# A two-block kernel on one core: the latent branch's projection as split products, its gating in pairs, and what moves between VectorE, ScalarE and GpSimd with it

## The chip, the cores and the metric

The kernel runs on one NeuronCore of a Trainium2 chip. The metric is the device time of one execution in microseconds (us); a measured time is the median of several runs. The engines are TensorE (PE in the rows; PEld is its weight load), VectorE (DVE), ScalarE (ACT), GpSimd (POOL) and SyncE (SP), which issues the transfers of weights. Each runs its own list of instructions in order and waits for the others on semaphores.

## What is computed

The reference runs two transformer blocks, one after the other, on 256 tokens of width 1024, all in float32. The part that the change touches is the mixer of the first block:

```python
proj = u @ w_in                                   # also g, the gates
o_a = dense_attention(q, k_a, v_a)                # latent branch, 8 heads of 64
o_b = dilated_mixture(qd, kd, vd)                 # dilated branch, 8 heads of 64
gates = sigmoid(g + b_gate)                       # 2 x 1024 per token
merged = gates[:, :, 0] * (o_a @ w_branch_a) + gates[:, :, 1] * (o_b @ w_branch_b)
mix = merged @ w_out
```

Before it stand a feed-forward block (SwiGLU) and the projections of the mixer; behind it a norm, a second feed-forward block, and then the second block with its own mixer of three branches.

## The kernel before

**Layout.** Activations lie transposed: 128 rows of a chunk of features by 256 tokens, eight chunks for the width. Weights come from one stream of tiles of 128 x 1024 floats (512 KB), which SP loads into a ring of six slots; a slot is loaded again when its tile has been used (`tiles_used`). The order of the stream is a list (`weight_order`). In the mixer it is: sixteen gate tiles `g1`, the four tiles `wb` of the dilated branch (the first of them ahead of the last gate tile), the four tiles `wa` of the latent branch, eight tiles `out1`, and then the feed-forward weights.

**Split products.** Nearly every product is made as three faster ones: each operand x is written as an upper part (x rounded to fp32r) and a lower part (x minus the upper), and `split_product` (L632 to L634) does upper by upper, upper by lower, lower by upper. Of a weight tile ScalarE makes the upper (`weight_upper`, L1546) into a place of its own, and GpSimd the lower (`weights_lower`, L2873), which it leaves in the ring. A table of places (`SPLIT_PLACE`) says where uppers go, and GpSimd walks the tiles in the order of the stream. The latent branch's four tiles `wa` are not split before the change: L994 multiplies whole float32 operands, four products for each of the eight chunks of 256 tokens.

**The head loop.** Sixteen heads (0 to 7 dilated, 8 to 15 latent) are worked in a software pipeline beside the sixteen gate tiles; step k of it handles gate tile k and head k. On PE a pair of steps is: gate tile 2n (24 products), the scores of heads 2n+2 and 2n+3 (L925), which wait until ScalarE has read the scores of the pair before (`exps`), the transposes of head 2n (L936), which wait for its probabilities (`probs`), the values of the pair before (L952), gate tile 2n+1, transposes of head 2n+1. On VectorE step k is: reciprocal of the sums of head k and scaling of its two halves of probabilities (`normalise`, L2392 and L2394), gate tile times the norm's inverse (L2429), the maxima of head k+2 (L2385, L2386), and in odd steps from 3 on the outputs of two heads out of PSUM (L2403 as a lower part for heads 0 to 7, L2406 as a copy for 8 to 15). On ScalarE: for heads 0 to 7 their upper parts, tanh of the gate (L1723), a weight upper or two (L1546), the copy of the transposes of head k (`turned`, L1704), and the exponentials of head k+2 (`exps`, L1696). The dilated branch's four projections are woven into the end of it (`dilated_branch`), each over a whole bank of 512 columns.

**The latent branch.** When the last dilated tile is done, PE works off eight products of 256 columns, m1_0 to m1_7, in two alternating banks. VectorE reads each with its gate (L2449), adds it to the dilated branch's chunk (L2452), and one chunk behind that makes the lower part for the next product (L2295), whose upper part ScalarE has made (L1553). PE then starts `out1`, the product with `w_out`: eight tiles of 24 products (192), where each chunk k of the first tile waits for the k-th pair of parts of `merged` (`input_parts`).

**GpSimd's order there.** After the lowers of all `g1` and `wb` tiles it sums the squares of the context's norm (`context_sums`, L2927 and L2928, three operations of 512 columns and one of 256), then makes the lowers of the eight `out1` tiles. The first use of the sum is behind the third `out1` tile on PE.

## Time and profile before

| | |
|---|---|
| median of 3 runs | 1250.64 us (1243.90 to 1254.69) |
| profiled execution | 1251.45 us |
| its span in the trace | 1249.8 us, 24409 instructions |
| PE, DVE, ACT, POOL busy | 95%, 68%, 51%, 44% of the span |
| mean granted clock of TensorE | 0.982 |

Times in the rows are us from the start of the span. A row of a timeline is: start, duration, engine, line and operation, out<-in, how many were merged into it, and in brackets the idle time ahead of it and what ended it. The durations of PE's rows overlap, since its products are pipelined; the distance of two starts is what one costs. A row of the windows is: the stretch, its length, for each engine busy time and number of instructions, the granted clock of TensorE (1.00 is 2.4 GHz, 0.50 is 1.2 GHz), the share of the DMA engines and GB/s.

### The profile page before, as it was taken

What the parts mean: (1) busy time and instruction counts of PE and PEld (TensorE: products, weight loads), DVE (VectorE), ACT (ScalarE), POOL (GpSimd) and SP (SyncE); (2) the same over time, 40 slices, a digit from 0 to 9 for tenths busy, and PEclk for the clock granted to TensorE, in tenths of its full rate; (3) what the DMA queues carried; (4) which work ended last, traced back from release to release, by engine and by line L of the source; (5) the groups of instructions that cost most, each with busy time, mean ns of one, the idle gap of its engine ahead of it and who ended that gap; (6) DMA issues with size and microseconds to landing.
All of it is one profiled execution on the core that took longest, in us unless ns stands there. A gap on an engine that the chain in (4) does not pass through costs nothing.

```text
span 1249.8 us, 24409 instructions
## 1 busy us (share of the span) xinstructions
PE 1193.5 (95%) x9116; PEld 1115.9 (89%) x9116; DVE 849.3 (68%) x1142; ACT 635.5 (51%) x1020; POOL 553.2 (44%) x287
## 2 busy tenths in 40 slices
PE   6999998999999999999999999998999999999998
PEld 6999998976888999999999888987777899999998
DVE  6798984864986567777554852688745686656555
ACT  5534446525773454545445546466425634655553
POOL 0355656732455433443435644468530384222331
PEclk9999998999999989999989999998999999999999
DMA  8677764433334547788514334232323264565653
GB/s 314 229 279 279 264 233 135 152 101 119 104 117 135 169 169 255 283 286 285 188 49 152 119 101 129 75 102 84 102 68 101 85 179 142 172 195 189 187 189 111
DMA packets 58096, 207.04 MB, mean 166 GB/s; under 512 B 6576, under 2 KB 8240, under 8 KB 57776
## 3 DMA queue, kind: packets, MB, share of 16 engines
q1 hardware_dynamic: 49824, 177.23, 43.4%
q0 software_dynamic: 6912, 25.17, 5.7%
q10 hardware_dynamic: 1296, 3.74, 0.8%
q8 instruction: 45, 0.74, 0.2%
q14 instruction: 19, 0.16, 0.0%
HBM read 205.07 MB, written 1.05 MB: 165 GB/s over the span
## 4 chain that ended last, share of the span: by engine, by line
PE 61%; DVE 19%; issue 6%; ACT 6%; POOL 4%; DMA 3%; DVEq 0%; SPq 0%; POOLq 0%; ACTq 0%
PE psum L632 17%; PE psum L633 16%; PE psum L634 16%; DVE parts L2143 4%; DMA low<-stream 3%; POOL own_parts L2873 2%; POOL high L2956 2%; DVE high L2174 1%; PE psum L771 1%; PE psum L925 1%; PE psum L643 1%; PE psum L645 1%; ACT parts L1477 1%; PE psum L657 1%; PE psum L644 1%
## 5 line engine op out<-in xcount | busy, mean ns | idle before, releaser
L632 PE MATMUL psum<-parts 128*128 128x256 f32 x1584 | 443.9, 280 | 19.7 <-DVE parts L2143 9.8
L633 PE MATMUL psum<-parts 128*128 128x256 f32 x1584 | 446.6, 282 | 0.0
L634 PE MATMUL psum<-parts 128*128 128x256 f32 x1584 | 442.5, 279 | 0.0
L632 PEld LDWEIGHTS psum<-parts 128*128 128x128 f32 x1584 | 300.3, 190 | 22.9 <-issue 16.7
L2881 POOL TENSOR_TENSOR parts<-low,parts 128x1024 fp32r<-128x1024 f32 x60 | 169.0, 2817 | 340.2 <-ACT parts L1477 340.2
L633 PEld LDWEIGHTS psum<-parts 128*128 128x128 f32 x1584 | 300.3, 190 | 0.0
L634 PEld LDWEIGHTS psum<-parts 128*128 128x128 f32 x1584 | 300.1, 189 | 0.0
L1477 ACT ACTIVATE parts<-low 128x1024 fp32r<-128x1024 f32 x198 | 205.5, 1054 | 129.3 <-DMA low<-stream 127.8
L2873 POOL TENSOR_TENSOR own_parts<-low,parts 128x1024 fp32r<-128x1024 f32 x75 | 184.5, 2472 | 166.9 <-ACT parts L1546 166.6
L2143 DVE TENSOR_TENSOR parts<-low,parts 128x1024 fp32r<-128x1024 f32 x138 | 178.9, 1331 | 23.3 <-ACT parts L1477 22.8
L633 PE MATMUL psum<-u_parts,parts 128*128 128x256 f32 (+1 forms) x560 | 164.5, 294 | 0.0
L634 PE MATMUL psum<-scratch_parts,own_parts 128*128 128x256 f32 (+1 forms) x496 | 149.6, 302 | 0.0
L2873 POOL TENSOR_TENSOR own_parts<-low,single_upper 128x1024 fp32r<-128x1024 f32 x36 | 88.9, 2474 | 82.1 <-ACT single_upper L1546 79.5
L633 PEld LDWEIGHTS psum<-u_parts,parts 128*128 128x128 f32 x560 | 107.7, 192 | 2.1
L634 PE MATMUL psum<-late_parts,own_parts 128*128 128x256 f32 x360 | 101.0, 281 | 0.0
L634 PEld LDWEIGHTS psum<-scratch_parts,own_parts 128*128 128x128 f32 x496 | 95.8, 193 | 3.7
L632 PE MATMUL psum<-late_parts,parts 128*128 128x256 f32 x320 | 92.6, 290 | 4.3 <-DVE u_parts L2283 3.1
L632 PE MATMUL psum<-scratch_parts,single_upper 128*128 128x256 f32 (+1 forms) x256 | 79.5, 311 | 6.9 <-POOL own_parts L2873 5.7
L1546 ACT ACTIVATE parts<-low 128x1024 fp32r<-128x1024 f32 x75 | 78.4, 1050 | 14.3 <-DMA low<-stream 14.3
L633 PE MATMUL psum<-u_parts,single_upper 128*128 128x256 f32 (+1 forms) x280 | 83.3, 298 | 0.0
L2174 DVE SCALAR_TENSOR_TENSOR high<-high,low 128x1024 f32<-128x1024 f32 x64 | 79.1, 1275 | 0.0
L2149 DVE TENSOR_TENSOR parts<-low,parts 128x256 fp32r<-128x256 f32 x66 | 54.9, 831 | 31.9 <-ACT parts L1483 31.9
(369 smaller groups left out, 2122.4 us busy)
## 6 DMA issues: line engine op xcount, KB each, us to landing
low<-stream SPq DMA_DIRECT2D x334, 512.0 KB, 3.5
high<-conditioning POOLq DMA_DIRECT2D x48, 512.0 KB, 5.1
high<-wuq ACTq DMA_DIRECT2D x1, 1152.0 KB, 11.2
low<-x SPq DMA_DIRECT2D x4, 256.0 KB, 5.8
high<-ctx ACTq DMA_DIRECT2D x1, 1024.0 KB, 5.6
out<-low SPq DMA_DIRECT2D x8, 128.0 KB, 1.8
low<-cst ACTq DMA_DIRECT2D x1, 850.5 KB, 4.9
low<-vec ACTq DMA_DIRECT2D x1, 157.5 KB, 5.7
```

Source lines behind the costliest of these rows:

```text
L632: pe.matmul(out, w_hi[:, cols_], x_hi, start=start, stop=False, **kw)
L633: pe.matmul(out, w_hi[:, cols_], x_lo, start=False, stop=False, **kw)
L634: return pe.matmul(out, w_lo[:, cols_], x_hi, start=False, stop=stop, **kw)
L643: pe.matmul(out, hi(k, n), w_hi[:, cols_], start=k == 0, stop=False)
L1477: act.activation(ring_hi[:, j % RING, :], ring[:, t % RING, :], ACT.Copy)\
L1546: act.activation(weight_place(t), ring[:, t % RING, :], ACT.Copy)\
L2143: dve.tensor_tensor(ring_lo[k][:, j % RING, :], ring[:, t % RING, :], ring_hi[:, j % RING, :], ALU.subtract).then_inc(S("lower_ready"), 1)
L2149: dve.tensor_tensor(hidden_lo[k][:, par, :], hidden[:, par, :], hidden_hi[k][:, par, :], ALU.subtract).then_inc(S("hidden_split"), 1)
L2174: dve.scalar_tensor_tensor(out=acc_, in0=cond_places[g], scalar=small[:, bass.ds(i * 2 + who, 1)], in1=acc_, op0=ALU.mult, op1=ALU.add).th ...
L2873: pool.tensor_tensor(tile_lo[:, t % RING, :], ring[:, t % RING, :], weight_place(t), ALU.subtract).then_inc(S("weights_split"), 1)
L2881: pool.tensor_tensor(ring_lo[k][:, j % RING, :], ring[:, t % RING, :], ring_hi[:, j % RING, :], ALU.subtract).then_inc(S("lower_ready_2"), 1)
L2956: pool.affine_select(out=a, in_=a, compare_op=ALU.is_ge, fill=NEG, base=0, pattern=[[-sgn * P, 2], [sgn, T]], channel_multiplier=-sgn)\
```

## The change

- The tiles `wa` are split: they get places 29 to 32 for their uppers (where the latent queries and keys stood), ScalarE makes four more uppers and GpSimd four more lowers, and one function `head_branch` now projects either branch with split products, two chunks into one bank. The eight banks m1_0 to m1_7 become four, wa_0 to wa_3.
- The outputs of heads 8 to 15 are split too: ScalarE writes their upper parts (`head_upper_1`), VectorE subtracts instead of copying.
- Gating, adding, uppers and lowers of the merged chunks go in pairs of 512 columns. The add's wait for its own result ahead of the lower is gone.
- For heads 12 to 15 ScalarE scales the probabilities (`normalised`, in steps 11 to 14 between tanh and the weight upper); VectorE only takes the reciprocal, behind the maxima of head k+2.
- GpSimd makes the context's sums in two pieces: two operations behind the lower of gate tile 12, the others behind the lower of the first `wb` tile. Ahead of the lower of the second `out1` tile it waits until three of the four pairs are merged.
- The gate rows before tanh lie in a buffer of their own (`gated_rows`), and two semaphores for memsets become one.

The diff, cut to its core:

```diff
 for tiles, places in (...
-                      (tiles_between(("g1", GATES_1[0]), ("wb", 3)), (5, 4) * 5 + (5, 26, 27, 4, 5, 28, 26, 27, 4, 5)),
+                      (tiles_between(("g1", GATES_1[0]), ("wa", 3)),
+                       (5, 4) * 5 + (5, 26, 27, 4, 5, 28, 26, 27, 4, 5, 29, 30, 31, 32)),
...
-            def dilated_branch(pair):
+            def head_branch(m, pair):
...
-                    pe.wait_ge(S("outs_copied"), 8)
-                w = split_weights(AT[("wb", pair)])
+                    pe.wait_ge(S("outs_copied"), 8 if m == "wb" else 16)
+                w = split_weights(AT[(m, pair)])
...
-            for n in range(8):
-                name = f"m1_{n}"
-                bank_free(pe, name)
-                w = tile_wait(AT[("wa", n // 2)])
...
-                    mm = pe.matmul(bank(name)[:, 0:T], w[:, (n % 2 * 4 + k) * P:(n % 2 * 4 + k + 1) * P], oa[:, k, :],
-                                   start=k == 0, stop=k == 3)
+            for pair in range(4):
+                head_branch("wa", pair)
...
+            def normalised(k):
+                x = 2 * (k % 2)
+                act.wait_ge(S("inverse_sums"), k - 11)
+                for j in range(2):
+                    act.activation(prob[:, k % 2, j, :], prob[:, k % 2, j, :], ACT.Identity, scale=rden[:, x + j:x + j + 1])\
+                       .then_inc(S("probs"), 1)
...
-                if k in (3, 5, 7, 9):
+                if k % 2 and k > 1:
...
+                if 10 < k < 15:
+                    normalised(k + 1)
...
-            merged_upper(merged1, "merged1", {0: [AT[("out1", 0)]], 1: [AT[("out1", 1)]], 3: [AT[("out1", 2)]],
-                                                7: [AT[("out1", 3)]]})
+            weight_upper(AT[("wa", 1)])
+            weight_upper(AT[("wa", 2)])
+            head_upper_1(14)
+            head_upper_1(15)
+            weight_upper(AT[("wa", 3)])
+            for pair in range(4):
+                if pair < 3:
+                    weight_upper(AT[("out1", pair)])
+                act.wait_ge(S("merged"), 2 * pair + 2)
+                act.activation(p1_hi[:, 2 * pair:2 * pair + 2, :], merged1[:, 2 * pair:2 * pair + 2, :], ACT.Copy)\
+                   .then_inc(S("input_uppers"), 2)
+            weight_upper(AT[("out1", 3)])
...
             for k in range(16):
-                normalise(k)
+                if k < 12:
+                    normalise(k)
...
                 if k < 14:
                     maxima(k + 2)
+                if 10 < k < 15:
+                    inverse_sums(k + 1)
...
+            for pair in range(4):
+                name, own = f"wa_{pair}", slice(2 * pair, 2 * pair + 2)
                 product_ready(dve, name)
...
+                dve.tensor_tensor(merged1[:, own, :], merged1[:, own, :], latent_gated, ALU.add).then_inc(S("merged"), 2)
+                if pair:
+                    merged_lower_1(pair - 1)
+            dve.wait_ge(S("merged"), 8)
+            merged_lower_1(3)
...
-            weights_lower(AT[("cq", 0)] + 5, AT[("wb", 3)])
-            context_sums()
-            weights_lower(AT[("out1", 0)], AT[("out1", 7)])
+            weights_lower(AT[("cq", 0)] + 5, AT[("g1", GATES_1[12])])
+            context_sums(1, 3)
+            weights_lower(AT[("g1", GATES_1[13])], AT[("wb", 0)])
+            context_sums(3, 5)
+            weights_lower(AT[("g1", GATES_1[15])], AT[("out1", 0)])
+            pool.wait_ge(S("merged"), 6)
+            weights_lower(AT[("out1", 1)], AT[("out1", 7)])
```

How ScalarE's list reads in steps 11 and 12 of the head loop. Before (L1723 is tanh, L1546 a weight upper, L1704 the copy of the transposes, L1696 the exponentials, L1431 a square of the context):

```order
L1723 ACTIVATE high<-high,low 128x256
L1546 ACTIVATE parts<-low 128x1024
L1704 ACTIVATE high<-psum 128x512
L1696 ACTIVATE high,low<-psum,low 128x256 x2
L1431 ACTIVATE low<-high 128x512
L1723 ACTIVATE high<-high,low 128x256
L1546 ACTIVATE single_upper_65<-low 128x1024
```

And now (L1726 is tanh, L1707 the upper parts of two latent heads, L1713 the scaling of a head's probabilities, L1542 a weight upper):

```order
L1707 ACTIVATE heads_latent_upper<-psum 64x256 x2
L1726 ACTIVATE high<-high,low 128x256
L1713 ACTIVATE high<-high,low 128x256 x2
L1542 ACTIVATE parts<-low 128x1024
L1700 ACTIVATE high<-psum 128x512
L1692 ACTIVATE high,low<-psum,low 128x256 x2
L1427 ACTIVATE low<-high 128x512
L1726 ACTIVATE high<-high,low 128x256
L1713 ACTIVATE high<-high,low 128x256 x2
L1542 ACTIVATE single_upper_65<-low 128x1024
```

The scaling of a head stands between tanh and the weight upper, so ahead of the exponentials on which PE's next scores wait.

The end of VectorE's part in the merge, from the last gating of the dilated branch on. Before, the last three of eight chunks (L2449 gates, L2452 adds, L2295 makes the lower part):

```order
L2449 SCALAR_TENSOR_TENSOR high<-high,psum 128x256
L2452 TENSOR_TENSOR high<-high 128x256
L2295 TENSOR_TENSOR u_parts<-high,late_parts 128x256
L2449 SCALAR_TENSOR_TENSOR high<-high,psum 128x256
L2452 TENSOR_TENSOR high<-high 128x256
L2295 TENSOR_TENSOR u_parts<-high,late_parts 128x256 x2
```

Now, the last two of four pairs (L2483 gates, L2487 adds, L2473 makes the lower part):

```order
L2483 SCALAR_TENSOR_TENSOR high<-high,psum 128x512
L2487 TENSOR_TENSOR high<-high 128x512
L2473 TENSOR_TENSOR u_parts<-high,late_parts 128x512
L2483 SCALAR_TENSOR_TENSOR high<-high,psum 128x512
L2487 TENSOR_TENSOR high<-high 128x512
L2473 TENSOR_TENSOR u_parts<-high,late_parts 128x512 x2
```

The same three kinds of operation, half as many and twice as wide; the last two lowers still stand behind the last add.

GpSimd's list from the lowers of gate tiles 11 and 12 on. Before (L2873 is a weight lower, L2927 and L2928 are the context's sums; the last row is the eight `out1` tiles):

```order
L2873 TENSOR_TENSOR own_parts<-low,single_upper_63 128x1024
L2873 TENSOR_TENSOR own_parts<-low,single_upper_64 128x1024
L2873 TENSOR_TENSOR own_parts<-low,parts 128x1024 x2
L2873 TENSOR_TENSOR own_parts<-low,single_upper_65 128x1024
L2873 TENSOR_TENSOR own_parts<-low,single_upper_63 128x1024
L2873 TENSOR_TENSOR own_parts<-low,single_upper_64 128x1024
L2873 TENSOR_TENSOR own_parts<-low,parts 128x1024 x2
L2927 TENSOR_TENSOR low<-low 128x512 x3
L2928 TENSOR_TENSOR low<-low 128x256
L2873 TENSOR_TENSOR own_parts<-low,parts 128x1024 x8
```

And now, from behind the lower of gate tile 12 on (L2908 is a weight lower, L2962 and L2964 the sums, single_upper_66 to 69 the tiles `wa`):

```order
L2962 TENSOR_TENSOR low<-low 128x512 x2
L2908 TENSOR_TENSOR own_parts<-low,parts 128x1024 x2
L2908 TENSOR_TENSOR own_parts<-low,single_upper_65 128x1024
L2962 TENSOR_TENSOR low<-low 128x512
L2964 TENSOR_TENSOR low<-low 128x256
L2908 TENSOR_TENSOR own_parts<-low,single_upper_63 128x1024
L2908 TENSOR_TENSOR own_parts<-low,single_upper_64 128x1024
L2908 TENSOR_TENSOR own_parts<-low,parts 128x1024 x2
L2908 TENSOR_TENSOR own_parts<-low,single_upper_66 128x1024
L2908 TENSOR_TENSOR own_parts<-low,single_upper_67 128x1024
L2908 TENSOR_TENSOR own_parts<-low,single_upper_68 128x1024
L2908 TENSOR_TENSOR own_parts<-low,single_upper_69 128x1024
```

The sums stand ahead of seven weight lowers of the head loop instead of behind them, and the four new lowers stand ahead of `out1`.

## Rows read from the trace of the kernel before

**Rows 1.** The page: busy time of the engines; the chain by engine

```profile
PE 1193.5 (95%) x9116; PEld 1115.9 (89%) x9116; DVE 849.3 (68%) x1142; ACT 635.5 (51%) x1020; POOL 553.2 (44%) x287
PE 61%; DVE 19%; issue 6%; ACT 6%; POOL 4%; DMA 3%; DVEq 0%; SPq 0%; POOLq 0%; ACTq 0%
```

**Rows 2.** Timeline of PE: latent projection, first and last tiles of out1

```profile
393.35 5.99 PE L994 MATMUL psum<-high,low 128*128 128x256 f32 x27
...
400.84 1.99 PE L994 MATMUL psum<-high,low 128*128 128x256 f32 x8 [0.42 <-DVE high L2449]
403.79 5.45 PE L994 MATMUL psum<-high,low 128*128 128x256 f32 x24 [0.96 <-DVE high L2449]
408.89 0.47 PE L632 MATMUL psum<-late_parts,parts 128*128 128x256 f32 x1
...
411.88 0.38 PE L632 MATMUL psum<-late_parts,parts 128*128 128x256 f32 x1
...
428.05 0.28 PE L634 MATMUL psum<-late_parts,own_parts 128*128 128x256 f32 x1
...
432.56 0.28 PE L634 MATMUL psum<-late_parts,own_parts 128*128 128x256 f32 x1
```

**Rows 3.** The chain in order of time: part of the latent projection

```profile
393.51 3.47 PE psum L994 x16
```

**Rows 4.** Timeline of VectorE and GpSimd in the merge

```profile
389.55 0.69 DVE L2413 SCALAR_TENSOR_TENSOR high<-high,psum 128x512 f32<-128x512 f32 x1 [2.54 <-PE psum L634]
393.55 0.69 DVE L2413 SCALAR_TENSOR_TENSOR high<-high,psum 128x512 f32<-128x512 f32 x1 [2.10 <-PE psum L634]
397.53 0.42 DVE L2452 TENSOR_TENSOR high<-high 128x256 f32<-128x256 f32 x1
397.99 2.47 DVE L2295 TENSOR_TENSOR u_parts<-high,late_parts 128x256 fp32r<-128x256 f32 x1
400.82 2.13 DVE L2452 TENSOR_TENSOR high<-high 128x256 f32<-128x256 f32 x1
...
388.04 4.01 POOL L2927 TENSOR_TENSOR low<-low 128x512 f32<-128x512 f32 x3
...
397.63 5.04 POOL L2873 TENSOR_TENSOR own_parts<-low,parts 128x1024 fp32r<-128x1024 f32 x2 [4.77 <-ACT parts L1546]
405.67 2.45 POOL L2873 TENSOR_TENSOR own_parts<-low,parts 128x1024 fp32r<-128x1024 f32 x1 [3.00 <-ACT parts L1546]
```

**Rows 5.** Timeline of the head loop, steps 13 and 14: VectorE, GpSimd, PE

```profile
374.10 4.70 DVE L2394 TENSOR_SCALAR high<-high,low 128x256 f32<-128x256 f32 x2
373.86 4.79 POOL L2873 TENSOR_TENSOR own_parts<-low,single_upper 128x1024 fp32r<-128x1024 f32 x2 [2.58 <-ACT single_upper L1546]
378.86 0.66 PE L936 MATMUL psum<-low,high 128*128 128x128 f32 x4 [1.03 <-DVE high L2394]
```

**Rows 6.** Timeline of the head loop, step 11: ScalarE, VectorE, GpSimd, PE

```profile
362.49 0.51 ACT L1723 ACTIVATE high<-high,low 128x256 f32<-128x256 f32 x1 [1.37 <-DVE high L2429]
362.90 1.04 ACT L1546 ACTIVATE parts<-low 128x1024 fp32r<-128x1024 f32 x1
363.08 0.58 DVE L2386 TENSOR_SCALAR low<-low 128x2 f32<-128x2 f32 x1
361.20 2.44 POOL L2873 TENSOR_TENSOR own_parts<-low,parts 128x1024 fp32r<-128x1024 f32 x1
365.39 1.99 PE L925 MATMUL psum<-high 96*128 96x256 f32 x8 [0.18 <-ACT high L1696]
```

**Rows 7.** Windows: TensorE's granted clock around gaps in its work

```profile
777.00:780.60 3.60, 1.77 (x16) 1.57 (x14) 2.27 (x2) 3.59 (x6) 1.24 (x2) 1.00 0.20 35
780.60:784.00 3.40, 3.40 (x16) 3.17 (x17) 0.00 (x0) 0.63 (x1) 2.35 (x1) 0.50 0.29 117
376.00:380.00 4.00, 2.97 (x26) 2.45 (x27) 3.93 (x6) 0.83 (x4) 2.65 (x2) 1.00 0.59 170
210.50:217.40 6.90, 4.24 (x20) 4.27 (x21) 6.22 (x14) 4.65 (x10) 6.27 (x8) 0.51 0.01 2
```

More of the change, by code:

```diff
@@ L267 @@
                  24: HEADS_M, 25: ARENA_2["ys"][0],
-                 26: ARENA_1["qd"][0], 27: ARENA_1["kd"][0], 28: ARENA_1["vd"][0]}
+                 26: ARENA_1["qd"][0], 27: ARENA_1["kd"][0], 28: ARENA_1["vd"][0],
+                 **{29 + i: ARENA_1["q"][0] + i * TILE for i in range(4)}}
 assert SINGLE_PLACES[18] + TILE <= ARENA_2["t0"][0]
@@ L302 @@
           + ["wb_0", f"g1_{GATES_1[15]}", "wb_1", "wb_2", "wb_3"]
-          + [f"m1_{n}" for n in range(8)]
+          + [f"wa_{n}" for n in range(4)]
           + ["rows", "mk0"] + [f"mq{n}" for n in range(4)] + ["ish"]
@@ L324, in tile_of @@
 def tile_of(name):
-    for m in ("g1_", "g2_", "wb_"):
+    for m in ("g1_", "g2_", "wb_", "wa_"):
         if name.startswith(m):
@@ L330, in tile_of @@
         return AT[("uk", 0)]
-    if name.startswith("m1_"):
-        return AT[("wa", int(name[3:]) // 2)]
     if name == "rows":
@@ L2921, in link, with context_sums @@
                 pool.wait_ge(S("pool_steps"), steps[0])
-            def context_sums():
-                for i in range(1, 4):
+            def context_sums(first, last):
+                for i in range(first, min(last, 4)):
                     pool.wait_ge(S("squares"), SQ_BASE["ctx"] + i + 1)
                     link(pool.tensor_tensor(tmp[:, 0:2, :], tmp[:, 0:2, :], tmp[:, 2 * i:2 * i + 2, :], ALU.add))
-                pool.tensor_tensor(tmp[:, 0, :], tmp[:, 0, :], tmp[:, 1, :], ALU.add).then_inc(S("square_sums_2"), 1)
+                if last == 5:
+                    pool.tensor_tensor(tmp[:, 0, :], tmp[:, 0, :], tmp[:, 1, :], ALU.add).then_inc(S("square_sums_2"), 1)
             pool.wait_ge(S("cond_ready"), 1)
```

101 lines of the change are left out of this document (54 added, 47 removed).

## The prediction

> **What bounds the kernel now.** I read the page first: PE is busy 95% of the span, and the chain runs through it for 61% and through VectorE for 19% [rows 1]. So a microsecond counts only where it shortens PE's list or a wait in it. Next the timeline of PE around the latent projection [rows 2]: it starts at 393.35, the first `out1` product at 408.89, the second `out1` tile at 411.88. From there PE runs to the last product of the eighth tile at 432.56 without a wait of note. What costs time here is thus the projection (15.54 us), the first tile behind it (2.99 us), and the waits in the head loop ahead of it. Of these I look at two: 1.03 us at 378.86 [rows 5] and 0.18 at 365.39 [rows 6]. Then the timelines of VectorE and GpSimd [rows 4], because the same operation of VectorE takes 0.42 us once and 2.13 another time. Last the windows for TensorE's clock [rows 7].
>
> **How VectorE and GpSimd share.** L2452 and L2295, 256 columns with both inputs in SBUF, take 0.42 us when GpSimd is idle. At 397.99 L2295 took 2.47, at 400.82 L2452 took 2.13: each ended 0.3 us behind the GpSimd operation that was running. The operation at 389.55, 512 columns with one input in PSUM, took its 0.69 us in the middle of GpSimd's sums [rows 4]. With two GpSimd operations back to back (373.86, 4.79 us) two scalings on VectorE took 4.70 us together: one gets through at the end of each GpSimd operation [rows 5]. I take this as the rule of the sum: an SBUF-only operation of VectorE waits for the end of the GpSimd operation under way, and the next GpSimd operation goes ahead of the next VectorE one.
>
> **The change part by part.**
>
> *Projection.* 96 split products replace 32 float32 ones. One split product costs 4.51/39 = 0.116 us (40 starts from 428.05 to 432.56 [rows 2]), a tile of 24 costs 2.77, the four 11.1 us. The float32 ones stand in the trace as 64 instructions of 3.47/16 = 0.217 [rows 3], 13.9 us, and their phase took 15.54 with its waits. The weights are there in time: the uppers of `wa` need about 1 us of ScalarE each (1.04, L1546 [rows 6]) and the lowers 2.4 to 2.5 us of GpSimd (2.45, L2873 [rows 4]), less than the 2.77 a tile takes on PE, and GpSimd can start on them where the sums began, at 388.04 [rows 4], so the fourth is done by 398.1 and is asked for at 393.35 + 3 x 2.77 = 401.7. Banks are read within 1 us of a tile's end. So 11.1 - 15.54 = **-4.4 us**. Bounds: -2.8 if only the passes are saved (11.1 - 13.9), -4.4 if the waits go too.
>
> *Merge in pairs.* Here the gain is put at risk. I count from the end of the third `wa` tile. VectorE starts 0.2 us behind a tile's end (the last dilated tile frees PE at 393.35 [rows 2], its gating starts at 393.55 [rows 4]). Gating and adding 512 columns cost 0.69 each (the row at 389.55 has 512 columns). So: gating 0.2 to 0.9, adding to 1.6. That is three pairs merged, and it releases GpSimd, which has had the uppers of its next two tiles waiting. VectorE's next operation, the lower of pair 1, is already issued and goes first, to 2.2; GpSimd's lower of `out1` tile 1 runs from 2.1 to 4.5. The fourth tile ends at 2.77, its gating (PSUM, free) at 3.7. The add needs both inputs from SBUF and waits: 4.5, done 5.05. GpSimd goes on with tile 2, 4.9 to 7.3; the lower of pair 2 waits for it, done 7.85. ScalarE has by then copied the upper of pair 3 (5.1 to 5.7) and made the upper of tile 3 (to 6.7), so GpSimd goes on with it, 7.7 to 10.1, and the lower of pair 3 is done at 10.65. PE ends its first `out1` tile six products later, at 11.4. From its start at 2.77 that is 8.6 us, of which 3.8 and 2.1 are waits, against 2.99 before: **+5.6 us**. Bounds: were GpSimd idle, the chain would be 0.2 + 0.69 + 0.69 + 0.7 + 0.7 us long, then six products, 3.8 us in all, **+0.8 us**; the upper bound is the one above, since after the fourth lower nothing is left to collide. I take the upper one: it is what the rows give in order.
>
> *Head loop, step 11.* In step 11 PE's scores at 365.39 wait for ScalarE: tanh at 362.49, weight upper at 362.90, copy, exponentials [rows 6]. Two scalings of 256 columns now stand behind that tanh, 0.41 us each as tanh itself (362.49 to 362.90). They also wait for the reciprocal, which stands behind the maxima of head 13. The last operation of those, L2386 at 363.08, ended at 363.66 with GpSimd's operation, not after its own 0.17 us or so [rows 6]; GpSimd now stands in the two sums that were put there. They take 1.3 us each (4.01/3 [rows 4]): from 361.3 to 363.95. Reciprocal to 364.1, scalings to 364.95, and the weight upper starts 2.05 us later than at 362.90. PE's scores come **+2.05 us** later. Without the collision (L2386 done at 363.25) it would be +1.4. The upper parts of heads 8 and 9 go into ScalarE's idle 1.37 us ahead of tanh, at no cost; if that cover were gone, 0.8 us. Queued behind ScalarE's new wait are the weight upper, the copy and the exponentials, in this order.
>
> *Head loop, step 14.* The scalings of head 14 on VectorE, 4.70 us beside GpSimd [rows 5], were what PE's transposes at 378.86 waited for. The wait shows as 1.03 us behind a product drawn with 0.28, which frees PE after 0.12; so **-1.2 us**. ScalarE has these scalings done some 3 us before PE asks. What is late next is nothing I can find: the lower of gate tile 15, by the same count, comes 1 to 2 us ahead of its use.
>
> *Sums on GpSimd.* They leave the stretch in front of `out1`, where their 4.7 us covered nothing, since `wa` was not split; their result is used behind the third `out1` tile. The four new lowers take their place. Nothing from it but what stands above.
>
> *TensorE's clock.* A gap of 1.83 us on PE ending at 780.38 was followed by 3.4 us at 0.50, 1.2 GHz; the gap of 1.03 us ending at 378.86 was not, 1.00 all through [rows 7]. The waits of 3.8 and 2.1 us in the first `out1` tile lie above it. While PE has work at 1.2 GHz it does half of it, so one such stretch costs 3.4/2 = **+1.7 us**. Bounds: 0, and 3.4 for a stretch as long as at 210.50 (6.9 us) [rows 7]. The Trainium skill (TensorE: Matmul & The Clock Gate, "What's actually happening") says that the half clock is the state at rest and that activity lifts it, and its table has it return after idleness. A strict reading, that only unbroken idleness brings it, would make this term fall away for gaps of 2 us; the trace disagrees, a gap of 1.83 us was enough.
>
> **The sum.** -4.4 + 5.6 + 2.05 - 1.2 + 1.7 = +3.8 us on the profiled 1251.45, 1255.3. The median shown is 0.8 below the profiled execution, so 1254.5 us. Nothing behind 432.56 changes but the moment at which it starts. About 1% (12.5 us) is what a measurement of this kernel can tell from no change; this is 0.3%, no change by that bound.
>
> **The rivals.**
>
> *GpSimd and VectorE do not fall into step.* For it: the upper of `out1` tile 3 is ready only 0.6 us before GpSimd could take it, and a VectorE operation that is issued at once may go first. Against it: 4.70 beside 4.79 us [rows 5]. Then the first tile takes 3.8 us, no clock stretch comes: -4.4 + 0.8 + 2.05 - 1.2 = -2.8, 1247.9 us by the median. If the reciprocal is not held up either, 0.65 less, 1247.2. The Trainium skill (SBUF — State Buffer, "Practical consequences") says that issue order decides who holds the ports, not the kind of operation; by that, whoever is issued first at each release decides between this rival and the forecast.
>
> *The gap in the head loop lowers the clock too.* PE would wait at 365.4 for 0.2 + 2.05 us, more than the 1.83 of rows 7. Another 3.4 us at half clock, +1.7: 1256.2 us.
>
> *ScalarE becomes the bound of the last steps (the slower side).* The scaling of each of heads 12 to 15 waits on a reciprocal behind VectorE's maxima, which wait for PE's scores, and delays the uppers, copies and exponentials behind it. I have charged one head. If all four delay PE by 2.05 and each brings a clock stretch of 1.7, that is 4 x 3.75 = 15 instead of 2.05, so +16.8, 1267.5 us. It decides once ScalarE has no idle time left in a step; it has 1.37 us in step 11 [rows 6], and its wait at tanh is for VectorE, which gets lighter. That speaks against it.
>
> *The change does not do what it says*: PE waits for the lowers of `wa`, and the projection takes 15.5 as before. Then +4.4: 1258.9 us. The 3.6 us in hand, worked out above, speak against it.
>
> **How the numbers follow.** Forecast 0.50; not in step 0.28; the gap with a clock stretch 0.13; ScalarE the bound 0.05; the rest 0.04. The range must hold the forecast, the first rival and the second, and the spread of executions (1243.90 to 1254.69 before, whose median may lie 2 us off): 1246 to 1260 leaves out the slowest rival and some of the spread. Faster by over 1% needs more than all gains without a loss (-4.4 - 1.2): 0.03. Slower by over 1% is ScalarE as the bound and a little more: 0.06. The rest, 0.91, is within 1%.
>
> **What would show it.** In the profile after: the projection on PE from its first to the first `out1` product some 11.1 us long, without float32 pairs. The last two lowers of the merge on VectorE over 2 us each, beside three GpSimd lowers back to back, and waits of PE in the first `out1` tile of about 3.8 and 2.1 us. PE's wait for the scores of heads 14 and 15 about 2 us, none ahead of the transposes of head 14. A clock of 0.50 for 3.4 us or more behind the merge. The prediction is wrong if the last two lowers take 0.7 us each, or if the wait for the scores stays below 1 us, or if ScalarE is late in steps 12 to 14 too.

## The result, and the profile after

The changed kernel takes 1255.32 us (median of 22 runs, 1250.16 to 1264.48), beside 1250.64 us for the kernel before (22 runs, 1241.80 to 1256.39). The ratio is 1.0041, its 95% interval 1.0023 to 1.0059. So the change costs 0.2 to 0.6% and is no difference by the bound of 1%; forecast were 1254.5 us and no change.

The profiled execution of the changed kernel took 1252.21 us. Its page, the busy times, the chain by engine, and the group of split products that wait for the merged chunks:

```profile
span 1249.3 us, 24483 instructions
PE 1189.1 (95%) x9148; PEld 1114.7 (89%) x9148; DVE 834.7 (67%) x1122; ACT 647.0 (52%) x1036; POOL 544.1 (44%) x291
PE 69%; DVE 13%; ACT 6%; issue 5%; POOL 4%; DMA 2%; DVEq 0%; POOLq 0%; SPq 0%; ACTq 0%
L634 PE MATMUL psum<-late_parts,parts 128*128 128x256 f32 x320 | 93.3, 291 | 9.3 <-DVE u_parts L2473 5.1
```

The span is 0.5 us shorter than before, although the runs are slower, and PE is busy 4.4 us less [rows 1]. Whoever compares these two totals alone reads a gain. The stages say where the error lies: PE's first product of the mixer starts at 207.4 us here and at 213.2 before, 5.8 us earlier, though nothing ahead of it was changed. Across the profiled executions of all kernels of this study, with the same code up to there, the mixer starts between 207.4 and 214.0. One profile can't be compared with another by its span when what is looked for is 4 us. I therefore read stage against stage. The last row gives the place: 5.1 us of PE's idle time in that group was ended by L2473, the lower part of the merged chunks.

**The latent branch.** The timeline of PE; what is named L632 before is L634 here.

```profile
388.08 0.28 PE L634 MATMUL psum<-heads_latent_upper,single_upper 128*128 128x256 f32 x1
...
399.17 0.28 PE L634 MATMUL psum<-late_parts,parts 128*128 128x256 f32 x1
...
404.29 0.39 PE L634 MATMUL psum<-late_parts,parts 128*128 128x256 f32 x1 [3.57 <-DVE u_parts L2473]
...
407.05 0.58 PE L634 MATMUL psum<-late_parts,parts 128*128 128x256 f32 x1 [1.52 <-DVE u_parts L2473]
...
408.50 0.41 PE L634 MATMUL psum<-late_parts,parts 128*128 128x256 f32 x1
```

The projection takes 399.17 - 388.08 = 11.09 us instead of 15.54 [rows 2], 4.45 less, and PE does not wait in it. The first `out1` tile, 24 products, takes 408.50 - 399.17 = 9.33 us. From one start to the next it is 3.85 us ahead of 404.29 and 1.93 ahead of 407.05.

How long the tile took before has to be counted, and [rows 2] can mislead: its row at 411.88 is not the second tile but the last chunk of the first. Between 408.89 and 411.88 stand only 21 products. The second tile starts three products later, and 24 products behind that the third:

```profile
412.33 0.28 PE L632 MATMUL psum<-late_parts,parts 128*128 128x256 f32 x1
...
415.12 0.28 PE L632 MATMUL psum<-late_parts,parts 128*128 128x256 f32 x1
```

So the first tile took 412.33 - 408.89 = 3.44 us before, not the 2.99 of the prediction, and it now takes 5.89 us more.

What it waits for, in the timelines of VectorE and GpSimd over the same time:

```profile
397.99 0.69 DVE L2473 TENSOR_TENSOR u_parts<-high,late_parts 128x512 fp32r<-128x512 f32 x1
399.37 0.69 DVE L2483 SCALAR_TENSOR_TENSOR high<-high,psum 128x512 f32<-128x512 f32 x1 [0.70 <-PE psum L636]
400.15 1.33 DVE L2487 TENSOR_TENSOR high<-high 128x512 f32<-128x512 f32 x1
401.40 5.59 DVE L2473 TENSOR_TENSOR u_parts<-high,late_parts 128x512 fp32r<-128x512 f32 x2
...
398.20 2.73 POOL L2908 TENSOR_TENSOR own_parts<-low,parts 128x1024 fp32r<-128x1024 f32 x1 [4.88 <-DVE high L2487]
400.89 2.79 POOL L2908 TENSOR_TENSOR own_parts<-low,parts 128x1024 fp32r<-128x1024 f32 x1
403.65 2.80 POOL L2908 TENSOR_TENSOR own_parts<-low,parts 128x1024 fp32r<-128x1024 f32 x1
```

The three GpSimd operations end at 400.93, 403.68 and 406.45. VectorE's three operations with both inputs in SBUF end at 401.48, 404.2 and 406.99, each half a microsecond behind one of them: one gets through per operation of GpSimd. The gating at 399.37, with one input in PSUM, takes its 0.69 in the middle of such an operation. The lower at 397.99, issued 0.2 us ahead of GpSimd's first, takes 0.69 too. That agrees with what the Trainium skill says of issue order (SBUF — State Buffer, "Who interferes with whom"): the operation that issues first is not held up.

**The head loop.** The timelines of ScalarE and PE in step 11, and of PE ahead of the scores:

```profile
356.32 0.51 ACT L1726 ACTIVATE high<-high,low 128x256 f32<-128x256 f32 x1 [0.72 <-DVE high L2451]
357.92 0.91 ACT L1713 ACTIVATE high<-high,low 128x256 f32<-128x256 f32 x2 [1.10 <-DVE low L2419]
358.74 1.04 ACT L1542 ACTIVATE parts<-low 128x1024 fp32r<-128x1024 f32 x1
...
361.36 1.99 PE L927 MATMUL psum<-high 96*128 96x256 f32 x8 [2.32 <-ACT high L1692]
```

ScalarE stands 1.10 us for the reciprocal (L2419), scales for 0.8, and starts the weight upper 2.42 us behind tanh, where it was 0.41 before [rows 6]: 2.0 later. PE waits 2.32 us for the scores instead of 0.18. The wait of 1.03 us ahead of the transposes of head 14 [rows 5] is gone.

**The clock.** Windows of the changed kernel behind the merge:

```profile
401.00:404.80 3.80, 0.51 (x4) 0.51 (x5) 3.80 (x3) 2.86 (x3) 3.80 (x2) 1.00 0.28 108
404.80:411.65 6.85, 5.33 (x25) 5.04 (x25) 4.93 (x4) 0.00 (x0) 1.65 (x1) 0.50 0.22 72
```

While PE waits the clock still reads 1.00. Half a microsecond after it resumes, the clock is at 0.50, 1.2 GHz, and stays there for 6.8 us. The last six products of the first tile and the first of the second run in it; tiles two to eight, up to the start of their last product, take 430.16 - 408.50 = 21.66 us, where they took 432.56 - 412.33 = 20.23 before and take 20.22 in those kernels below whose clock stays up.

### The profile page after: what moved, and what is told of

Same layout as the page of the kernel before. It is cut to its first block, busy times and chain, and to the rows that moved or that the text cites. A ratio compares the mean times of both kernels' runs of the same rounds, so it can differ in the third digit from the quotient of the medians.

```text
span 1249.3 us, 24483 instructions
## 1 busy us (share of the span) xinstructions
PE 1189.1 (95%) x9148; PEld 1114.7 (89%) x9148; DVE 834.7 (67%) x1122; ACT 647.0 (52%) x1036; POOL 544.1 (44%) x291
## 4 chain that ended last, share of the span: by engine, by line
PE 69%; DVE 13%; ACT 6%; issue 5%; POOL 4%; DMA 2%; DVEq 0%; POOLq 0%; SPq 0%; ACTq 0%
PE psum L634 20%; PE psum L635 19%; PE psum L636 19%; POOL own_parts L2908 2%; POOL high L2996 2%; DMA low<-stream 1%; PE psum L927 1%; PE psum L645 1%; PE psum L659 1%; PE psum L647 1%; PE psum L646 1%; DVE parts L2162 1%; DVE high L2614 1%; POOL low L2948 1%; ACT parts L1542 1%
## 5 line engine op out<-in xcount | busy, mean ns | idle before, releaser
L634 PE MATMUL psum<-parts 128*128 128x256 f32 x1584 | 440.9, 278 | 17.3 <-DVE parts L2162 10.1
L634 PEld LDWEIGHTS psum<-parts 128*128 128x128 f32 x1584 | 299.2, 189 | 18.7 <-issue 17.5
L2916 POOL TENSOR_TENSOR parts<-low,parts 128x1024 fp32r<-128x1024 f32 x60 | 149.8, 2497 | 350.8 <-ACT parts L1473 350.8
L2908 POOL TENSOR_TENSOR own_parts<-low,parts 128x1024 fp32r<-128x1024 f32 x75 | 184.6, 2475 | 161.6 <-ACT parts L1542 156.5
L2162 DVE TENSOR_TENSOR parts<-low,parts 128x1024 fp32r<-128x1024 f32 x138 | 163.5, 1218 | 22.7 <-ACT parts L1473 22.1
L2908 POOL TENSOR_TENSOR own_parts<-low,single_upper 128x1024 fp32r<-128x1024 f32 x40 | 98.3, 2467 | 85.4 <-ACT single_upper L1542 82.7
L634 PE MATMUL psum<-late_parts,parts 128*128 128x256 f32 x320 | 93.3, 291 | 9.3 <-DVE u_parts L2473 5.1
L634 PE MATMUL psum<-scratch_parts,single_upper 128*128 128x256 f32 (+1 forms) x256 | 79.9, 312 | 6.9 <-POOL own_parts L2908 5.7
L1542 ACT ACTIVATE parts<-low 128x1024 fp32r<-128x1024 f32 x75 | 78.3, 1051 | 15.8 <-DMA low<-stream 14.6
L2168 DVE TENSOR_TENSOR parts<-low,parts 128x256 fp32r<-128x256 f32 x66 | 60.9, 923 | 31.9 <-ACT parts L1479 31.9
```

Source lines behind the costliest of these rows:

```text
L634: pe.matmul(out, w_hi[:, cols_], x_hi, start=start, stop=False, **kw)
L1542: act.activation(weight_place(t), ring[:, t % RING, :], ACT.Copy)\
L2162: dve.tensor_tensor(ring_lo[k][:, j % RING, :], ring[:, t % RING, :], ring_hi[:, j % RING, :], ALU.subtract).then_inc(S("lower_ready"), 1)
L2168: dve.tensor_tensor(hidden_lo[k][:, par, :], hidden[:, par, :], hidden_hi[k][:, par, :], ALU.subtract).then_inc(S("hidden_split"), 1)
L2908: pool.tensor_tensor(tile_lo[:, t % RING, :], ring[:, t % RING, :], weight_place(t), ALU.subtract).then_inc(S("weights_split"), 1)
L2916: pool.tensor_tensor(ring_lo[k][:, j % RING, :], ring[:, t % RING, :], ring_hi[:, j % RING, :], ALU.subtract).then_inc(S("lower_ready_2"), 1)
```

## The experiments

Beside each ratio I set what the trace gives: the length of the head loop (from the first scores to the first product of the latent projection) and of what follows (from there to the last product of the eighth `out1` tile): 91.0 + 39.2 us before, 91.9 + 42.1 after.

### The merge: whose operations hold the lowers up

*a_nowait* takes GpSimd's new wait away:

```diff
-            weights_lower(AT[("g1", GATES_1[15])], AT[("out1", 0)])
-            pool.wait_ge(S("merged"), 6)
-            weights_lower(AT[("out1", 1)], AT[("out1", 7)])
+            weights_lower(AT[("g1", GATES_1[15])], AT[("out1", 7)])
```

> GpSimd no longer waits for three merged pairs ahead of the second out1 tile's lower. Theory (a VectorE operation with both inputs in SBUF waits for the end of the GpSimd operation under way): GpSimd makes the lowers of out1 tiles 1 and 2 earlier, from about 395.6 on the changed kernel's clock, one or two of VectorE's adds and lowers collide with them, but GpSimd has nothing left when the last add is due, so the last three run in 0.7 us each. The first out1 tile on PE then takes about 5.5 us instead of 9.35, and the stretch at half clock behind it may go: total 3.8 to 7 us below the changed kernel. Rival (the waits in the first out1 tile come from the longer chain of paired, twice as wide operations through VectorE and ScalarE, not from GpSimd): the tile stays at 9 us or above and the total at 1255.

*a_wait8* holds GpSimd back until all four pairs are merged:

```diff
-            pool.wait_ge(S("merged"), 6)
+            pool.wait_ge(S("merged"), 8)
```

> GpSimd waits for all four merged pairs instead of three. Theory: the last add is free (0.7 us instead of 1.3), the lower of pair 2 goes ahead of GpSimd (0.7), only the lower of pair 3 waits for one GpSimd operation (2.4 to 2.8 us). First out1 tile about 5.9 us instead of 9.35, one wait of PE of about 2.5 us; total about 3.4 to 6 us below the changed kernel. Rival (the chain's length alone): tile at 9 us or above, total at 1255.

*a_split* gives GpSimd the second tile ahead of the wait, and the rest only when all lowers of the merged chunks are made:

```diff
-            weights_lower(AT[("g1", GATES_1[15])], AT[("out1", 0)])
-            pool.wait_ge(S("merged"), 6)
-            weights_lower(AT[("out1", 1)], AT[("out1", 7)])
+            weights_lower(AT[("g1", GATES_1[15])], AT[("out1", 1)])
+            pool.wait_ge(S("input_parts"), INPUT_PARTS["merged1"] + DC)
+            weights_lower(AT[("out1", 2)], AT[("out1", 7)])
```

> GpSimd makes the lower of out1 tile 1 without a wait and waits for all eight parts of merged ahead of tile 2. Theory: that lower runs at about 395.6 to 398 beside one add at most, and no GpSimd operation stands beside the last add and the last two lowers. First out1 tile 3.8 to 4.5 us instead of 9.35 (5 us less), no stretch at half clock behind it: total 5 to 8 us below the changed kernel, about 1248. Rival (the chain's length alone): 9 us, 1255.

Measured: the first tile took 6.11, 6.11 and 4.09 us. Timeline of VectorE and GpSimd in a_nowait, then in a_wait8, then in a_split; the L2473 rows are the lowers in question:

```profile
401.57 2.85 DVE L2473 TENSOR_TENSOR u_parts<-high,late_parts 128x512 fp32r<-128x512 f32 x1
405.72 0.69 DVE L2473 TENSOR_TENSOR u_parts<-high,late_parts 128x512 fp32r<-128x512 f32 x1
406.66 0.69 DVE L2473 TENSOR_TENSOR u_parts<-high,late_parts 128x512 fp32r<-128x512 f32 x1 [0.25 <-ACT late_parts L1762]
398.15 5.72 POOL L2908 TENSOR_TENSOR own_parts<-low,parts 128x1024 fp32r<-128x1024 f32 x2 [2.30 <-ACT parts L1542]
407.56 2.39 POOL L2908 TENSOR_TENSOR own_parts<-low,parts 128x1024 fp32r<-128x1024 f32 x1 [3.69 <-ACT parts L1542]
```

```profile
404.59 0.68 DVE L2473 TENSOR_TENSOR u_parts<-high,late_parts 128x512 fp32r<-128x512 f32 x1
405.53 2.51 DVE L2473 TENSOR_TENSOR u_parts<-high,late_parts 128x512 fp32r<-128x512 f32 x1 [0.26 <-ACT late_parts L1762]
404.81 7.81 POOL L2908 TENSOR_TENSOR own_parts<-low,parts 128x1024 fp32r<-128x1024 f32 x3 [8.12 <-DVE high L2487]
```

```profile
409.58 0.68 DVE L2473 TENSOR_TENSOR u_parts<-high,late_parts 128x512 fp32r<-128x512 f32 x1
410.52 0.69 DVE L2473 TENSOR_TENSOR u_parts<-high,late_parts 128x512 fp32r<-128x512 f32 x1 [0.26 <-ACT late_parts L1762]
404.46 2.67 POOL L2908 TENSOR_TENSOR own_parts<-low,parts 128x1024 fp32r<-128x1024 f32 x1 [2.31 <-ACT parts L1542]
```

Where a GpSimd operation is under way or issued first, the lower takes 2.5 to 2.9 us; where none is, 0.69. The chain is the same in all kernels, so its length is not the cause; the rival falls. In a_wait8 the lower at 404.59 was issued 0.2 us ahead of GpSimd and passed, as at 397.99 above. The change's own wait for three merged pairs thus did harm: it released three of GpSimd's lowers just as VectorE's last add and last two lowers were due, and without it (a_nowait) the tile is 3.2 us shorter. One step of 1.06 us is left in a_split: that is the chain itself.

In time: a_nowait 1249.51 us, ratio 1.0001 (0.9972 to 1.0031); a_wait8 1251.11, 0.9996 (0.9978 to 1.0014); a_split 1248.59, 1.0003 (0.9974 to 1.0032). None can be told from the kernel before. a_wait8 had a stretch of 3.4 us at half clock behind its second wait, the two others none there. All three head loops took 93.6 us, 1.7 more than the changed kernel's in its own profile. The window of a_nowait behind its wait for the scores says why:

```profile
363.30:366.70 3.40, 3.40 (x13) 2.43 (x11) 0.76 (x2) 0.23 (x1) 0.55 (x1) 0.50 0.03 11
```

The gap of 2.6 us (from start to start) brought 3.4 us at half clock. It did so in five of the seven executions with this gap, and in two not, the first profile of the changed kernel among them (in the other, h_sums, the gap was 2.3 us).

### The head loop

*h_order* puts the scaling behind the exponentials:

```diff
-                if 10 < k < 15:
-                    normalised(k + 1)
...
                 if k < 14:
                     exps(k + 2)
+                if 10 < k < 15:
+                    normalised(k + 1)
```

> ScalarE scales heads 12 to 15 behind the exponentials of the same step instead of between tanh and the weight upper. Theory (the scaling and its wait for the reciprocal delay the exponentials on which PE's scores of heads 14 and 15 wait): the step between PE's last gate product and those scores falls from 2.60 us to 0.5 or less, no new wait ahead of the transposes of heads 12 to 15 (0.4 us at most each), total about 2 us below the changed kernel. Rival (the sums on GpSimd, by holding up the maxima, make the gap alone): it falls by 0.7 us at most.

```profile
366.44 1.78 PE L927 MATMUL psum<-high 96*128 96x256 f32 x7 [0.32 <-ACT high L1692]
```

That is PE's wait for the scores in its timeline: 0.32 us instead of 2.32; the head loop takes 89.9 us, the shortest so far. The merge is that of the changed kernel (9.33 us, half clock for 6.8 behind it), and the time is 1253.03 us, ratio 1.0009 (0.9980 to 1.0039).

*h_dve* leaves the scaling of all sixteen heads on VectorE:

```diff
-                if k < 12:
-                    normalise(k)
+                normalise(k)
...
-                if 10 < k < 15:
-                    inverse_sums(k + 1)
```

(and no `normalised` on ScalarE).

> VectorE scales heads 12 to 15 again, all else as in the changed kernel. Theory: the step ahead of the scores of heads 14 and 15 falls from 2.60 us to 0.6 to 1.0 (what is left is the maxima held up by the sums), and the wait ahead of the transposes of head 14, gone in the changed kernel, is back with a step of about 1.3 us. Total 0.5 to 1 us below the changed kernel, not to be told by the time alone. Rival (the sums on GpSimd make the gap): the step stays above 2 us.

Timeline of VectorE, GpSimd and PE in h_dve; line numbers are a few lower than in the changed kernel:

```profile
363.86 3.92 DVE L2411 TENSOR_SCALAR high<-high,low 128x256 f32<-128x256 f32 x2
360.16 2.67 POOL L2957 TENSOR_TENSOR low<-low 128x512 f32<-128x512 f32 x2
362.90 4.72 POOL L2903 TENSOR_TENSOR own_parts<-low,parts 128x1024 fp32r<-128x1024 f32 x2
367.83 0.66 PE L938 MATMUL psum<-low,high 128*128 128x128 f32 x4 [1.46 <-DVE high L2411]
379.51 0.66 PE L938 MATMUL psum<-low,high 128*128 128x128 f32 x4 [1.03 <-DVE high L2411]
```

A miss in part. The wait for the scores is gone, as expected, and the old wait for head 14 is back. But the total is no better than the changed kernel's: 1255.57 us, ratio 1.0035 (1.0005 to 1.0066). A new wait stands at 367.83: the sums at 360.16 push the two weight lowers behind them to 362.90, right beside the scalings of head 12, which take 3.92 us. So the parts of the change hang together. The scaling on ScalarE is what makes the sums in this place cheap for VectorE; the fault is only where on ScalarE it stands.

*h_sums* keeps the scaling on ScalarE and puts all sums behind the lower of the first `wb` tile:

```diff
-            weights_lower(AT[("cq", 0)] + 5, AT[("g1", GATES_1[12])])
+            weights_lower(AT[("cq", 0)] + 5, AT[("wb", 0)])
             context_sums(1, 3)
-            weights_lower(AT[("g1", GATES_1[13])], AT[("wb", 0)])
             context_sums(3, 5)
```

> GpSimd makes all the context's sums behind the lower of the first wb tile, none behind that of gate tile 12. Theory: the maxima of head 13 are held up less or as long as before by the lower of gate tile 13, so the step ahead of the scores of heads 14 and 15 falls from 2.60 to between 1.9 and 2.4 us; the sums' part in it is 0.7 us at most. Rival (the sums make the gap): it falls below 1 us. Total within 1 us of the changed kernel.

```profile
357.12 0.58 DVE L2405 TENSOR_SCALAR low<-low 128x2 f32<-128x2 f32 x1
355.24 2.44 POOL L2908 TENSOR_TENSOR own_parts<-low,parts 128x1024 fp32r<-128x1024 f32 x1
361.25 0.92 PE L927 MATMUL psum<-high 96*128 96x256 f32 x3 [2.00 <-ACT high L1692]
376.02 0.36 PE L634 MATMUL psum<-late_parts,single_upper 128*128 128x256 f32 x1 [0.88 <-POOL own_parts L2908]
```

These are rows of the timelines of VectorE, GpSimd and PE. The wait for the scores shrinks from 2.32 to 2.00 only. The last operation of the maxima (L2405) takes 0.58 us where it took 0.91 beside the sums, because a weight lower now stands where they stood (355.24 to 357.68). The larger part of the wait is the scaling itself, ahead of the exponentials. In turn the lower of the last gate tile, now behind four sums, comes late, at 376.02. 1256.16 us, ratio 1.0030 (0.9998 to 1.0062): nothing gained.

*h_undo* leaves of the change only the projection and the merge in pairs: it is h_dve with all the sums behind the lower of the first `out1` tile, where the kernel before has them ahead of it:

```diff
-            weights_lower(AT[("cq", 0)] + 5, AT[("g1", GATES_1[12])])
+            weights_lower(AT[("cq", 0)] + 5, AT[("out1", 0)])
             context_sums(1, 3)
-            weights_lower(AT[("g1", GATES_1[13])], AT[("wb", 0)])
             context_sums(3, 5)
-            weights_lower(AT[("g1", GATES_1[15])], AT[("out1", 0)])
             pool.wait_ge(S("merged"), 6)
```

> The changed kernel with both of its parts in the head loop undone: VectorE scales heads 12 to 15, and the context's sums stand behind the lower of out1 tile 0, where GpSimd waits. Theory: the head loop is as before the change, 91.0 us from the first scores to the first latent product instead of 91.9, with a step of 1.3 us ahead of the transposes of head 14 and none of 2 us ahead of scores; the merge is as long as in the changed kernel or up to 1.3 us longer, for the sums now stand beside an add. Rival (the two parts save time in the head loop): above 91.9.

1255.89 us, ratio 1.0042 (1.0014 to 1.0069); head loop 91.2 us, as before the change. The first tile took 10.51 us, with steps of 4.83 and 1.54, since GpSimd's sums now stand beside the adds too; and the clock fell already during the first wait, at 409.47, and stayed at half for 10.2 us. So the projection as split products with a paired merge, on its own and with the sums there, costs about what the whole change costs (+4.5 us by the two stages, +3.8 and +5.8 for the changed kernel). What moving the sums away saves in the merge, the late scores take back in the head loop. No run here has the split projection with a merge in single chunks, so how much of the cost comes from the pairing is not shown.

### The clock

*awake* gives PE work where it would wait: 30 products of 128x256 ahead of the fifth chunk of the first tile and 14 ahead of the seventh, into a free half bank that nothing reads.

```diff
+            def merged_ready(k):
+
+                if k in (4, 6):
+                    stay_awake({4: 30, 6: 14}[k], p1_hi)
+                pe.wait_ge(S("input_parts"), INPUT_PARTS["merged1"] + k + 1)
```

> The changed kernel with products that nobody reads (into a free half bank) put on TensorE where it waits in the first out1 tile: 30 ahead of chunk 4, 14 ahead of chunk 6. They add products and leave nothing of the computation out. Theory (the 3.4 to 6.8 us at half clock behind the merge come from the two waits): no stretch at half clock between 395 and 425 us, the first out1 tile still 9 us, the seven behind it in 20.2 us instead of 21.7 as in the changed kernel; total 1.5 to 2.5 us below the changed kernel. Rival (the clock would have fallen anyway): tiles 1 to 7 at 21.6, total as the changed kernel or longer.

*after_again* is the changed kernel once more, on the same chip.

> The changed kernel once more, as the neighbour of the others of this call on the same chip: 1255 us, 0.3 to 0.5% above the kernel before; first out1 tile 9.3 us.

The windows of awake over its first tile and over tiles two to eight:

```profile
407.89:416.67 8.78, 8.56 (x71) 8.16 (x69) 8.20 (x5) 2.87 (x3) 7.37 (x3) 1.00 0.26 81
416.67:436.89 20.22, 20.22 (x178) 20.22 (x177) 7.14 (x13) 10.23 (x17) 9.47 (x4) 1.00 0.56 173
```

The first tile is as long as the lowers make it (8.78 us), but PE has work in it, the clock stays at 1.00, and tiles two to eight take 20.22 us; in after_again they took 21.95, in its first tile of 9.33. The two waits thus cost 0.6 + 1.7 = 2.3 us beyond their own length, in clock alone (0.6 + 1.4 = 2.0 in the first profile of the changed kernel). In time: awake 1251.90 us, ratio 1.0015 (0.9984 to 1.0046), after_again 1255.79 us, ratio 1.0021 (0.9986 to 1.0056). The 3.9 us between the medians point the same way, though more than 2.3 and within what the intervals leave open; the windows are the evidence.

### A version that beats both

*best* is a_split and h_order together, *best_again* the same kernel on another chip, *best2* is best with the sums of h_sums.

> Both mends together: scaling behind the exponentials, and GpSimd's lower of out1 tile 1 free, the rest behind all eight parts of merged. Theory: step ahead of the scores of heads 14 and 15 at 0.6 us, first out1 tile 4.1 us, no half-clock stretch between 355 and 430 us. Against the changed kernel 2.0 + 5.2 us, and 1.7 to 3.4 for each of up to two half-clock stretches: total 1246 us, 4 to 5 below the kernel before. If the two do not add up, it stays at 1248.6, the time with the second mend alone.

> Both mends together once more: 1244 to 1247 us if the first result holds, 0.3 to 0.6% below the kernel before; first out1 tile 4.1 to 4.7 us, head loop 89.9 us from the first scores to the first latent product.

> As the last one, with all the context's sums behind the lower of the first wb tile. Theory: the sums hold up nothing on the path once the scaling stands behind the exponentials, so gap, tile and total are as in the last one, within 1 us. Rival (the sums cost on their own): 0.7 us or more below it.

The window of best from the first `out1` product to the last of the eighth tile, and PE's only wait in it:

```profile
401.23:426.20 24.97, 23.84 (x202) 23.26 (x201) 11.46 (x19) 13.74 (x21) 14.21 (x6) 1.00 0.56 170
```

```profile
404.18 0.38 PE L634 MATMUL psum<-late_parts,parts 128*128 128x256 f32 x1 [1.01 <-DVE u_parts L2473]
```

best took 1244.87 us, ratio 0.9940 (0.9909 to 0.9971), and best_again 1245.68, ratio 0.9949 (0.9921 to 0.9978): faster than the kernel before by about half a per cent, on two chips, which is under the bound of 1% too. best_again is 10.1 us faster than the changed kernel measured beside it (after_again, 1255.79). The first tile takes 4.71 us, not 4.1, because one lower of VectorE, at 397.27 beside GpSimd's operation at 396.93, took 2.89 us. best2 took 1248.74 us, ratio 0.9975 (0.9946 to 1.0005). It has a new wait of 0.55 us for a scaling ahead of the transposes at 373.28, and no gain to set against it: 0.8 us by the stages. The medians lie 3.9 us apart where 1 was expected, but the intervals overlap.

### All kernels by stage

| kernel | head loop | latent projection and out1 | both, against before | as a ratio | measured ratio |
|---|---|---|---|---|---|
| before | 91.0 | 39.2 | | | |
| changed | 91.9 | 42.1 | +3.8 | 1.0030 | 1.0041 |
| after_again | 93.6 | 42.4 | +5.8 | 1.0046 | 1.0021 |
| a_nowait | 93.6 | 37.4 | +0.8 | 1.0007 | 1.0001 |
| a_wait8 | 93.6 | 38.8 | +2.2 | 1.0017 | 0.9996 |
| a_split | 93.6 | 35.4 | -1.2 | 0.9990 | 1.0003 |
| h_order | 89.9 | 42.5 | +2.2 | 1.0018 | 1.0009 |
| h_dve | 92.8 | 42.0 | +4.6 | 1.0036 | 1.0035 |
| h_sums | 92.5 | 42.0 | +4.3 | 1.0034 | 1.0030 |
| h_undo | 91.2 | 43.6 | +4.5 | 1.0036 | 1.0042 |
| awake | 93.6 | 40.1 | +3.5 | 1.0028 | 1.0015 |
| best | 89.9 | 36.0 | -4.3 | 0.9966 | 0.9940 |
| best_again | 89.9 | 36.0 | -4.3 | 0.9966 | 0.9949 |
| best2 | 90.7 | 36.0 | -3.5 | 0.9972 | 0.9975 |

Times are us of each kernel's profiled execution. The difference is worked out from the two rounded columns, and the ratio beside it is 1 plus it over 1250.64 us. Two stages of one execution give the measured ratio within its interval for all kernels but one (a_wait8, 1.0017 beside 0.9978 to 1.0014), whereas the rest of the same executions, their spans without the two stages, scatters from 1112.0 to 1126.4 us. Nothing outside these two stages is needed to explain the result, though intervals this wide would also hide a microsecond or two.

The clock of all runs, not only the profiled ones, points the same way. The mean granted clock is 0.978 over the changed kernel's 22 runs and 0.981 to 0.982 over the 31 to 35 runs of the kernel before that stand beside each group of experiments. If every stretch below full clock is at 0.50, that is an estimated 55 us per execution at half clock against 46 to 47. The 8 to 10 us more fit the 6.8 us behind the merge and the 3.4 us in the head loop, which five of the six profiled executions with its gap of 2.6 us have.

## Why the prediction was right

Step by step, in the order of the sum:

- *Projection, -4.4.* 15.54 to 11.09, -4.45. Right, and for the reason given: 96 products at 0.116 us and no wait for a lower of `wa`.
- *Merge in pairs, +5.6.* +5.89. The mechanism came out to the tenth, the sum did not. The term is 8.6 - 2.99, and the 2.99 is a misreading of [rows 2]: the tile took 3.44 us, so the working gives +5.2, and the bound for an idle GpSimd +0.4 instead of +0.8. From the end of the third `wa` tile (388.08 + 3 x 2.77 = 396.4) the fourth pair's add was to be done after 5.05 us and was after 5.1; the two last lowers after 7.85 and 10.65, and were after 7.8 and 10.6. The waits were to be 3.8 and 2.1 and were 3.85 and 1.93. The tile was to take 8.6 us and took 9.33. What was missing is the clock: the half clock starts at 404.80, inside the first tile, so its last products cost more, 0.6 us (9.33 beside awake's 8.78). I had priced the stretch only as one behind the waits.
- *Head loop, step 11, +2.05.* The weight upper starts 2.0 us later, PE's wait grew from 0.18 to 2.32: +2.1. h_sums shows the split between scaling and collision: without the sums beside the maxima the wait is 0.3 us shorter, not 0.65, because another operation of GpSimd takes their place.
- *Head loop, step 14, -1.2.* The wait is gone; the head loop as a whole grew by 0.9 = 2.1 - 1.2.
- *The clock, +1.7.* Tiles two to eight: 21.66 and 21.95 us (changed and after_again) against 20.22 at full clock, +1.4 and +1.7, with the 0.6 above 2.0 to 2.3 in all. The stretch at 0.50 was 6.8 us long, twice what I took, but its first part lies over the second wait and costs nothing: 4.6 us of it are left behind 407.05. The cost stands between the value chosen (1.7) and the upper bound (3.4); this term was set a little low.

Together the stages give +3.8 us in the first profile and +5.8 in the second, and the medians +4.7; the sum was +3.8. The agreement to the tenth is luck. The misread tile made the sum 0.45 us too large; with 3.44 it would have been +3.35 and the forecast 1254.0. The clock's term was 0.3 to 0.6 us too small and hid that. And the first profile is one without the half clock in the head loop; after_again, the same kernel, has it.

The first rival (not in step, 0.28) fell: both lowers took 2.8 us. What decides it is the order of issue to 0.2 us: in a_wait8 a lower issued 0.2 us ahead of GpSimd passes it. The second rival, a half clock behind the head loop's gap (0.13), was in truth more likely than the forecast: it came in five of the seven profiled executions that have the gap, and then the head loop took 93.6 us, 1.7 more, exactly its price. The prediction gives no reason for so low a chance. The wait that it priced, 2.25 us, was longer than the 1.83 of [rows 7] that was followed by a stretch; on that row alone the case was open, not unlikely. ScalarE as the bound did not come: in the changed kernel's head loop PE waits for it over 0.6 us only in step 11 and ahead of the second pair of scores (1.38 us at 301.64), where it did before the change too (1.37). That PE would wait for the lowers of `wa` did not come either.

## What to carry to other kernels

An operation of GpSimd that is "off the path" is on it when VectorE's operation on the path has to wait it out. In the kernel before, single operations were held too (2.47 and 2.13 us [rows 4]), but PE still had products of the projection to work off. With the shorter projection the last two lowers, each behind a whole GpSimd operation, fell where PE had nothing else. Giving GpSimd one tile's lower ahead and holding it back until VectorE's were made shortened the tile from 9.33 to 4.09 us, and PE waited for no weight behind it (a_split: tiles two to eight in 20.22 us). When work moves to another engine, put it behind what that engine owes to the bound engine (the exponentials), not in the first gap (behind tanh). Judge a change of 0.3% by the stages it touches: two numbers from one trace told more here than the median of ten runs. And count the products when you mark where a stage ends: a row that looks like the start of a tile can be a chunk within one.

## What the runs showed of the hardware

- All gaps here are from start to start. After a gap of 2.6 us in TensorE's work its clock fell to 0.50 for 3.4 us in five executions and not in a sixth, the changed kernel's first profile, with the same code in the head loop. The 2.27 us of h_sums were not followed by a fall; a_wait8's second gap of 2.08 was, and so was that of [rows 7], which is 2.10 us so counted (1.83 of it idle). Not followed by one were 1.06 and 1.29 us (a_split, best), a_nowait's 1.80 and 1.29 close together, and the 1.84 us ahead of 367.83 in h_dve. Between 2.08 and 2.6 us the length of a gap alone did not tell whether the clock falls.
- GpSimd pays for the collisions too, but little: its lower takes 2.40 us with VectorE out of the way and 2.67 to 2.94 beside held-up operations of 512 columns, while VectorE's 0.69 becomes 2.5 to 2.9 when it waits out a whole one.
- The code behind the eighth `out1` tile, the same in all kernels, took 812.9 to 823.2 us in the 14 profiled executions. The time at half clock in it differs too; less half of that time it is 799.3 to 802.5 us, so the clock accounts for most of the scatter there.
- The first feed-forward block, the same code in all kernels, took 207.4 to 214.0 us from one execution to another. What makes it vary was not tried and stays open, as do two remainders: awake gained more by the medians than by its stages, and a_wait8 stayed below its stage sum.
